# ScalarE takes the gelu and weight of an expert slot one TensorE group after VectorE's dot

## The reference, cut to what matters

```python
u = jnp.take(w_u, idx, axis=0)
act = jax.nn.gelu(jnp.einsum('nhkd,nd->nhk', u, xb).astype(jnp.float32), approximate=False)
v = jnp.take(w_v, idx, axis=0)
return jnp.einsum('nhk,nhkd->nd', (g * act).astype(xb.dtype), v)
```

## Time and profile before

| | us |
|---|---|
| median of three runs | 2622.94 |
| lowest, highest | 2609.85, 2630.68 |
| the profiled execution | 2617.25 |
| its span, first to last instruction | 2615.4 |
| TensorE busy | 2019.9 (77%) |
| VectorE busy | 1734.0 (66%) |
| ScalarE busy | 972.8 (37%) |
| GpSimd busy | 936.7 (36%) |

### The profile page before, as it was taken

One profiled execution on the slowest core, in us unless ns is written; L12 is line 12 of the kernel. 1 busy time (PEld: TensorE's weight loads), 2 busy tenths in 40 slices (PEclk: granted clock), 3 DMA queues, 4 the chain that ended last, 5 costly groups with the idle time before them and its releaser, 6 DMA issues. The chain is left out here.

```text
span 2615.4 us, 27311 instructions
## 1 busy us (share of the span) xinstructions
PE 2019.9 (77%) x6925; PEld 1109.9 (42%) x6925; DVE 1734.0 (66%) x3917; ACT 972.8 (37%) x2489; POOL 936.7 (36%) x806
## 2 busy tenths in 40 slices
PE   6978897856666798787499786887867778787776
PEld 2667745745555533375255222322223222232222
DVE  3632278776766688728588677777776767776664
ACT  1412144353333334312433344444444434344443
POOL 0020022542222223203132564556555545454454
PEclk9998999978888899888699999999999999899999
DMA  8835678841121488858588999999999999999997
GB/s 321 287 137 179 228 292 309 302 162 65 65 81 49 192 329 346 314 200 328 194 349 335 401 421 397 412 422 422 421 408 412 421 391 404 388 414 417 392 418 296
DMA packets 113319, 805.69 MB, mean 308 GB/s; under 512 B 12596, under 2 KB 14006, under 8 KB 17046
## 3 DMA queue, kind: packets, MB, share of 16 engines
q0 software_dynamic: 93760, 680.96, 65.0%
q1 hardware_dynamic: 17704, 118.17, 12.3%
q10 hardware_dynamic: 1712, 4.98, 0.5%
HBM read 800.79 MB, written 3.28 MB: 307 GB/s over the span
## 5 line engine op out<-in xcount | busy, mean ns | idle before, releaser
L1131 POOL DMA_INDIRECT RG<-in_uv,idxs x264 | 346.0, 1311 | 522.9 <-DVE pl L1382 280.5
L903 ACT ACTIVATE agel<-apre 128x1 f32<-128x1 f32 x640 | 129.1, 202 | 957.6 <-DVE apre L1354 952.9
L559 PE MATMUL pl<-RG,BP 128*128 128x512 f32 x576 | 295.0, 638 | 106.8 <-ACT BP L919 106.0
L559 PE MATMUL pl<-RING,BP 128*128 128x512 f32 x576 | 289.6, 637 | 77.8 <-ACT BP L919 76.1
L584 PE MATMUL pa<-HL,RING 128*128 128x512 f32 (+2 forms) x960 | 317.6, 489 | 9.8 <-DVEq L416 6.5
L1354 DVE CUSTOM_DVE_ANT_0 R<-RG,AB 128x1024 f32<-128x1024 f32 x201 | 246.2, 1228 | 98.8 <-DMA RG<-in_uv,idxs 78.7
L1131 POOL DMA_INDIRECT RING<-in_uv,idxs x168 | 230.3, 1371 | 208.3 <-PE pl L559 134.7
L1354 DVE CUSTOM_DVE_ANT_0 R<-RING,AB 128x1024 f32<-128x1024 f32 x168 | 206.0, 1226 | 113.6 <-DMA RING<-in_uv,idxs 73.7
L584 PEld LDWEIGHTS pa<-HL,RING 128*128 128x128 f32 x960 | 167.5, 198 | 152.2 <-issue 118.4
L559 PEld LDWEIGHTS pl<-RG,BP 128*128 128x128 f32 x576 | 100.5, 193 | 293.5 <-ACT BP L919 218.8
L559 PEld LDWEIGHTS pl<-RING,BP 128*128 128x128 f32 x576 | 108.3, 200 | 253.1 <-ACT BP L919 156.5
(11 more groups left out here) (256 smaller groups left out, 3187.3 us busy)
## 6 DMA issues: line engine op xcount, KB each, us to landing
RING<-in_in_slabs SPq DMA_DIRECT2D x42, 1024.0 KB, 5.0
RING<-in_pq_slabs SPq DMA_DIRECT2D x24, 1152.0 KB, 6.0
RING<-in_ada_slabs SPq DMA_DIRECT2D x16, 1024.0 KB, 5.2
RING<-in_out_slabs SPq DMA_DIRECT2D x12, 1024.0 KB, 4.8
RG<-in_col_slabs POOLq DMA_DIRECT2D x8, 1024.0 KB, 7.0
RING<-in_o_slabs SPq DMA_DIRECT2D x8, 1024.0 KB, 6.0
RG<-in_uv,idxs POOLq DMA_INDIRECT x297, 12.3
RING<-in_uv,idxs POOLq DMA_INDIRECT x168, 14.6
```

The source lines that it names most:

```text
L559: last = nc.tensor.matmul(acc[:, c * 512:(c + 1) * 512], DG[:, k % 2, :], bufs[k % len(bufs)][:, D + c * 512:D + (c + 1) * 512], start=Fal ...
L903: A(agel[:, par, k:k + 1], apre[:, par, k:k + 1], ACT.Gelu).then_inc(gel_done, 1)
L1131: nc.gpsimd.indirect_dma_start(out=bufs[b], out_offset=None, in_=uv, in_offset=bass.IndirectOffsetOnAxis(ap=idxs[:, par, k:k + 1], axis=0) ...
```

## The change

`Beside` gets a third number, `late`, which is 1 for ScalarE and 0 for the other engines. With it a slot's place is one further in the list of groups, but never beyond the next slot's place. The last slot of each of the two ranges (127 and 191) keeps its own.

```diff
-            def __init__(self, slot, shift):
-                self.slot, self.shift, self.next, self.first, self.end = slot, shift, 0, 0, 0
+            def __init__(self, slot, shift, late=0):
+                self.slot, self.shift, self.late, self.next, self.first, self.end = slot, shift, late, 0, 0, 0
 
             def place(self, n):
                 n += self.shift
+                if self.late and n + 1 < self.end:
+                    return min(SLOT_AT[n] + self.late, SLOT_AT[n + 1])
                 return SLOT_AT[max(n, self.first)] if n < self.end else len(NAMES)
@@
             beside = Beside(lambda n: w_slot(n, n // TOPK, n % TOPK, n // TOPK % 2, n // TOPK != PH - 1,
-                                           n >= TSLOT and n % 2 == 1), 0)
+                                           n >= TSLOT and n % 2 == 1), 0, 1)
```

## The result

The changed kernel takes 2628.4 us (median of 12 runs, 2623.97 to 2644.41); the kernel before takes 2621.36 us (median of 12, 2609.85 to 2630.77). The ratio is 1.0035, 95% interval 1.0019 to 1.0051: 9.2 us slower, between 5.0 and 13.4. The forecast was +14.2 us, just above that interval. The profiled execution took 2628.54 us, its span is 2626.7 (before 2617.25 and 2615.4).

The account below looks back on a forecast made before the run. It took DMA to bound the last stage, VectorE with gathers the projections and mix, TensorE the query part. Terms -3.6 + 2.9 + 4.2 + 3.1 + 7.6 = +14.2 us on 2617.25 gave 2631.5, as a median 2637; range 2608 to 2660.

Parts of the forecast that it names:

- projections (0 to 51): Projections: slots and evictions still alternate, and VectorE with its gathers sets the pace; 0 us.
- entry (51 to 52): Entry into the merged stage: an earlier eviction lets transposes and the scan's first matmul start earlier; -3.6 us, from -5 to 0.
- beat of slot 53: Merged stage: slot 53's load, gelu and weight come ahead of an eviction TensorE already waits for; 1.7 us lost.
- slots 65 and 68: Merged stage, two later beats: the next head's transposes run within a microsecond of the eviction; 0.7 and 0.5 us lost.
- mix and what follows (69 to 128): Entry into the mix: VectorE's update waits 3.2 us for slot 73, one more load at slot 85; +4.2 us, bounds 0 to 8.
- norm and transposes (128 to 152): Last three tiles: two diagonals 2.4 us later each, against 1.7 us gained at square roots; +3.1 us, bounds -2 and +8.
- query part (152 to 196): Last post stage: TensorE waits 1.9 us for each of four odd slots' diagonals; +7.6 us, bounds 3.8 to 12.
- in steady state nothing moves in time: Projections: TensorE only gets one group further ahead while VectorE with its gathers sets the pace; 0 us.
- the small waits of VectorE on ScalarE: Ahead of the entry into the merged stage: VectorE's waits that might come back, the -5 us end of that term's range.
- first rival: All TensorE's waits for evictions are on the path, so 61.2 us come back: 2562 us; chance 5%.
- the 5 us that I had named as a sign of error: Merged stage: the prediction is wrong if this stage changes by more than 5 us either way.
- VectorE would become the bound of the query part: Rival: five even slots make VectorE wait 5.8 us each, 29 us on top: 2666 us; chance 12%.

Follow-up runs that it names:

- even_post: The changed kernel with odd slots from 129 on put back as in the kernel before; 2620.04 us, ratio 0.9988.
- split53: The kernel before with slot 53 alone one group later and the router's exp for tile 4 taken behind slot 52; 2622.93 us, one run.
- lag3_post: The kernel before with ScalarE one group later from slot 128 on and TensorE's diagonal three slots behind its dot, not two; 2612.21 us, ratio 0.9965.
- post_only: The kernel before with ScalarE one group later only for slots from 128 on; 2630.52 us, ratio 1.0026.

## Why the prediction was right, and where it was off

The sum was +14.2 us, measured are +9.2 (5.0 to 13.4). In stretches, as means of the profiles with either order (for slots 65 and 68 only of the six profiles at a granted clock of 0.84; over all fourteen the late order is 2.2 us shorter, which goes with the clock):

| term | forecast | measured |
|---|---|---|
| projections (0 to 51) | 0 | -7.2 |
| entry (51 to 52) | -3.6 | -0.4 |
| beat of slot 53 | +1.7 | +4.2 |
| slots 65 and 68 | +1.2 | +0.5 |
| mix and what follows (69 to 128) | +4.2 | +4.5 - 0.9 |
| norm and transposes (128 to 152) | +3.1 | +4.3 |
| query part (152 to 196) | +7.6 | +6.3 |
| sum | +14.2 | +11.3 |

That the sum comes out within 3 us is in part luck: the projections and the entry gained 4.0 us more than forecast, the beat of slot 53 lost 2.5 us more. The -0.9 behind the mix is the one long stretch of the kernel before.

**Query part: right in mechanism, place and size.** Four waits were forecast at slots 157, 167, 179 and 189, 1.9 us each. They are there, at 1.82. They sum to 7.3 us, of which 6.3 show in this table. Cut at TensorE's first query matmul and not at the dot of slot 152, the same profiles give +2.2 for the norm and +8.3 for the query part. Putting the odd slots back or moving the diagonals took them away, which shows the cause.

**Norm and transposes: right.** The two diagonals were forecast 2.4 us later; the waits grew from 4.22 to 6.65 and from 4.51 to 6.66, 2.4 and 2.2 us. VectorE's wait for slot 146's weight is 6.71 us (forecast 6), for slot 150's 12.95. even_post adds that these waits of VectorE cost little.

**Projections: the step that failed is "in steady state nothing moves in time".** I looked at the dots and gathers of VectorE, found these late, and gave 0. VectorE also has other work there, which needs ScalarE's evictions, and it waited 7.1 us for them in six places. The prediction had them as "the small waits of VectorE on ScalarE" and only as an end of a range, -5. Its sentence against the first rival, that an eviction ahead of a late dot does not make the dot earlier, is the same error. The 3.5 us at the scan's first matmul came as forecast, but not at the entry: the dot of slot 51 was 3.1 us early already (5.0 counted from the dot of slot 0), and VectorE's own wait for that matmul only shrank from 3.62 to 3.25.

**Merged stage: the term of slot 53 was mis-sized.** The wait of 1.7 us that I took is what the slot alone makes (split53: 0.43 to 2.13). I left out that slot 53 carries the router's exp, though I counted it for slot 85. In the changed kernel the wait is 3.85 us. With slots 65 and 68 the stretch 52 to 69 is 5.7 us longer in the two profiles, beyond the 5 us that I had named as a sign of error.

ScalarE's busy time grew by 10.8 us (972.8 to 983.6), about nine loads of 1.28 us. The traces have 205 and 214 loads where the prediction counted 175 and 184; the difference of nine is right. The page's row for the loads ahead of gelu (busy, mean ns, idle ahead of them), of which there were 94 before:

```profile
L905 ACT ACT_TABLE_LOAD x100 | 128.3, 1283 | 12.5 <-ACT HG L1053 3.0
```

A hundred loads have 12.5 us of idle ahead of them, 0.13 us each, and behind a load the next instruction starts at once (above, the load of 601.06 ends at 602.34 and the exp starts at 602.36). The Trainium skill, ScalarE: Activation LUTs, section What ACT_TABLE_LOAD costs, adds 1.38 us of drain to each; no such time stands before or behind these loads, and the measurement decides for 1.28.

**Mix: about right, for another reason than given.** The wait of VectorE for slot 73 is 2.85 us (forecast 3.2), but by slot 77 VectorE is no later than before: it had waited 1.95 us for a gather there. Waits for the weights of slots 85 to 87 of 0.73, 1.13 and 1.07 us follow, and yet at slot 95 VectorE is only 0.4 us later than before, counted from slot 69. The loss comes at slot 96, where VectorE waits 3.88 us for a gather in place of 1.04, and grows to 5.5 us by slot 127. Why that gather takes longer, and what adds the last 2.2 us, is open.

**Rivals.** The first, 61.2 us back, is out. That VectorE would become the bound of the query part is out as well: from 1309 to 1450 it waits 25.3 us for weights, of which 12.95 belong to slot 150 ahead of the first query group, so 12.4 are left (before 5.0), less than half of the 29 that the rival counted. even_post has 10.7 of them and loses nothing, so its idle time was usable.

## What to carry to other kernels

Behind which group an engine takes a side job is worth what the reader of that job's result does while it waits: a reader that works in order and has no slack (TensorE here, with 130.55 of 131 us) pays the full latency, and one with idle time pays little. Whoever moves a producer later must move the strict consumer too; here the two moves together won 9 us where each alone lost 7 or won nothing. And when a slot is moved, move or leave out what hangs on it: the router's exp behind slot 53 cost more than all else in that stage.

## What the runs showed of the hardware

From slot 54 to slot 69 TensorE has the same 1018 matmuls in every kernel, and still the stretch took from 252.5 to 263.6 us. In lag3_post and in post_only, which have the same order of all engines there:

```profile
613.45:866.03 252.58, 164.66 (x1018) 141.89 (x1018) 167.95 (x393) 88.84 (x165) 56.37 (x81) 0.84 0.18 63
```

```profile
611.13:874.69 263.56, 178.76 (x1018) 153.09 (x1018) 168.82 (x393) 88.95 (x165) 56.07 (x81) 0.79 0.18 60
```

The 1018 matmuls are the same, the granted clock is 0.84 and 0.79, and TensorE's busy time 164.66 and 178.76 us. All six profiles of 252.5 to 253.2 us have 0.84, the eight longer ones 0.79 to 0.83, in either order. Between the two rows above no other engine's busy time differs by more than 0.9 us. So this stage, with short matmuls and gaps between them, scatters by 11 us together with the clock, more than this change is worth, and two single profiles can't be compared over it. What decides the clock from one execution to the next is not shown. A second event of this kind is the 90.16 us of the kernel before from slot 127 to 128, where thirteen other profiles take 82.9 to 86.5; its 424 matmuls take 68.31 us at a granted clock of 0.84, those of the changed kernel 64.16 at 0.89, and it holds a wait for a slab of weights, behind which the next group took 2.67 us where the groups before it take 1.95:

```profile
1155.10 2.67 PE L584 MATMUL pa<-HL,RING 128*128 128x128 f32 x16 [2.08 <-DMA RING<-in_pq_slabs]
```

In the beat of slot 53 the longer wait also cost clock: behind 3.85 us of standing idle the six transposes took 2.04 us at a granted clock of 0.50, behind 2.13 us they took 1.11 at 1.00.
